# Attention steps of a two-layer mixer block: output banks, placement of weight splits, gates on GpSimd and an earlier first reciprocal

## What is computed

```
p = norm(x) @ w_in ; split: a (u, v, z), b (q, k, v, z), c (q, k, v, o, z, gates)
a: gelu(u) * (w_s @ layer_norm(gelu(v)) + b_s) * silu(z)
b: softmax(rope(norm(q)) . rope(norm(k)) * scale) @ v * silu(z)     8 heads, 2 kv heads
c: h = chunkwise mLSTM in both directions; norm(h) * g_head * sigmoid(o) * silu(z)
x = x + mod * (concat(a, b, c) @ w_out)
```

## Time and profile before

| | us |
|---|---|
| median of 3 runs | 1150.38 (1149.53 to 1152.26) |
| the profiled execution | 1150.57 |
| its span | 1148.6 |
| PE busy | 1093.4 (95%) |
| VectorE, ScalarE, GpSimd busy | 722.2, 590.7, 130.0 |
| mean granted clock of PE | 0.987 |
| attention of layer 0 | about 211 to 292 |
| attention of layer 1 | about 464 to 508 |

### The profile page before, as it was taken

The page is one execution under the profiler, slowest core; times in us unless marked ns, Lnnn a source line. Parts: engine busy times, 40 slices in busy tenths (PEclk is TensorE's granted clock), DMA queues, the critical chain, the costliest instruction groups (busy, mean ns, idle before and its releaser), DMA issues.

```text
span 1148.6 us, 19921 instructions
## 1 busy us (share of the span) xinstructions
PE 1093.4 (95%) x8128; PEld 958.1 (83%) x8128; DVE 722.2 (63%) x1227; ACT 590.7 (51%) x969; POOL 130.0 (11%) x156
## 2 busy tenths in 40 slices
PE   3999999999989999889999999999998999999998
PEld 1787888766767989579888999999997789999997
DVE  4546557376434667766866667666676667766764
ACT  5343666445233567656556555444465536544443
POOL 0000000044020000233223100000012321000000
PEclk9999999999898999989999999999999999999999
DMA  9732112177420433014433345555543233555451
GB/s 371 268 137 79 68 43 74 41 278 270 147 74 1 160 144 116 33 55 157 179 125 114 144 147 221 184 185 182 184 149 119 101 115 143 200 187 200 182 187 54
DMA packets 24426, 167.01 MB, mean 145 GB/s; under 512 B 2832, under 2 KB 3216, under 8 KB 4752
## 3 DMA queue, kind: packets, MB, share of 16 engines
q1 hardware_dynamic: 24336, 165.74, 39.4%
HBM read 164.68 MB, written 1.05 MB: 144 GB/s over the span
## 4 chain that ended last, share of the span: by engine, by line
PE 86%; DVE 5%; ACT 4%; issue 2%; POOL 1%; DMA 1%; SPq 0%; DVEq 0%; ACTq 0%; POOLq 0%
PE bank L426 24%; PE bank L427 23%; PE bank L428 23%; DVE wlo L420 2%; ACT whi L405 2%; PE bank L464 2%; PE bank L1373 2%; PE bank L1506 1%; PE bank L1526 1%; PE bank L1516 1%; PE bank L1400 1%; PE bank L1391 1%; DMA raw<-in_stream 1%; PE bank L479 1%; PE bank L2455 1%
## 5 line engine op out<-in xcount | busy, mean ns | idle before, releaser
L426 PE MATMUL bank<-OPH,whi 128*128 128x256 f32 (+1 forms) x1716 | 526.5, 307 | 5.8 <-DVE wlo L420 3.4
L427 PE MATMUL bank<-OPL,whi 128*128 128x256 f32 (+1 forms) x1716 | 516.7, 301 | 0.0
L428 PE MATMUL bank<-OPH,wlo 128*128 128x256 f32 (+1 forms) x1716 | 516.5, 301 | 0.0
L420 DVE TENSOR_TENSOR wlo<-raw,whi 128x1024 fp32r<-128x1024 f32 x256 | 305.3, 1234 | 109.5 <-ACT whi L405 109.3
L426 PEld LDWEIGHTS bank<-OPH,whi 128*128 128x128 f32 x1716 | 329.3, 192 | 27.8 <-issue 7.6
L427 PEld LDWEIGHTS bank<-OPL,whi 128*128 128x128 f32 x1716 | 329.4, 192 | 12.5 <-issue 1.7
L428 PEld LDWEIGHTS bank<-OPH,wlo 128*128 128x128 f32 x1716 | 329.2, 192 | 11.5
L405 ACT ACTIVATE whi<-raw 128x1024 fp32r<-128x1024 f32 x256 | 255.6, 1049 | 103.8 <-PE bank L428 103.8
L426 PE MATMUL bank<-whi,OPH 128*128 128x256 f32 (+1 forms) x272 | 89.2, 328 | 0.0
L427 PE MATMUL bank<-wlo,OPH 128*128 128x256 f32 (+1 forms) x272 | 87.3, 321 | 0.0
L428 PE MATMUL bank<-whi,OPL 128*128 128x256 f32 (+1 forms) x272 | 87.1, 320 | 0.0
(11 more groups left out here) (284 smaller groups left out, 1167.1 us busy)
## 6 DMA issues: line engine op xcount, KB each, us to landing
raw<-in_stream SPq DMA_DIRECT2D x147, 1024.0 KB, 4.8
PROJ<-in_stream SPq DMA_DIRECT2D x5, 1024.0 KB, 14.9
X<-in_x_in SPq DMA_DIRECT2D x4, 512.0 KB, 6.3
C<-in_con SPq DMA_DIRECT2D x1, 1477.5 KB, 9.1
out<-PROJ SPq DMA_DIRECT2D x4, 256.0 KB, 2.0
WST<-in_w_s SPq DMA_DIRECT2D x2, 256.0 KB, 5.0
PROJ<-in_last_gain SPq DMA_DIRECT2D x1, 512.0 KB, 5.7
BS<-in_b_s SPq DMA_DIRECT2D x1, 256.0 KB, 5.3
```

The source lines that it names most:

```text
L420: nc.vector.tensor_tensor(c.w[1][:, part], c.raw[:, part], c.w[0][:, part].bitcast(F32), ALU.subtract).then_inc(*raises(c.lo[h]))
L426: nc.tensor.matmul(out, w[0], x[0], start=start, stop=False, skip_group_check=skip)
L427: nc.tensor.matmul(out, w[0], x[1], start=False, stop=False, skip_group_check=skip)
L428: return nc.tensor.matmul(out, w[1], x[0], start=False, stop=stop, skip_group_check=skip)
```

## The change

1. The last weighted sums go to score banks: `last_outs` gives blocks 14 and 15 of layer 0 banks 2 and 3, and blocks 5 and 6 of layer 1 banks 2 and 3.
2. Splits of the output projection: in layer 0 to s + 0.5 in step 15 as before, to s + 1 behind the whole of step 17, to s + 2 behind the whole of step 20 (the last). In layer 1 to s + 2 behind the whole of step 11 (before: inside step 7); step 12 is the last.
3. The recurrent gates: cz x co is done by GpSimd (`join_gates`), in layer 0 after norm(2), in layer 1 after norm(0). `gate` is then one product for each j. In layer 0 the two stand behind step 3 and behind step 4; in layer 1 both in `between` of step 1, as one instruction each that reads the bank and multiplies by g_head and by the joined gates; `give` is dropped there.
4. `invert_first` puts the reciprocal of layer 1's block 0 into step 0, ahead of the gmlp gate.

```diff
-                if n >= self.steps - 2:
-                    split(e, self.after.s + (n - self.steps + 3) / 2)
+                if n == self.steps - 2:
+                    split(e, self.after.s + 0.5)
...
+                self.last_outs, self.inverted = {}, 0
...
-                    self.O.append(OPAIR.take("pe", ("dve",)))
+                    self.O.append(self.last_outs.get(i, OPAIR).take("pe", ("dve",)))
...
+            def invert_first(self):
+                self.inverted = 1
+                stage(f"{self.name}_first").dve = lambda e: self.invert(e, 0)
...
-                if 1 <= j <= self.n:
+                if self.inverted < j <= self.n:
                     self.invert(e, j - 1)
...
-                self.ready = [[("c_gated", l, j)] for j in range(2)]
+                self.ready = [self.bank[j].freed if l else [("c_gated", l, j)] for j in range(2)]
...
+            def join_gates(self):
+                st, l, n = stage(f"recurrent{self.l}_gates"), self.l, self.n
+
+                def pool(e):
+                    for point in due(e, self.pr.ready("cz", "co")):
+                        e.wait_ge(*point)
+                    for j in range(2):
+                        z, o = proj(CZ + j)[:, 0, 0:n], proj(CO + j)[:, 0, 0:n]
+                        nc.gpsimd.tensor_tensor(z, z, o, ALU.mult).then_inc(*raises(("c_gates", l, j)))
+
+                st.pool = pool
...
-            def gate(self):
+            def gate(self, js=(0, 1)):
                 st, l, n = stage(f"recurrent{self.l}_gate"), self.l, self.n
 
                 def dve(e):
-                    for j in range(2):
-                        for point in due(e, self.bank[j].freed, self.pr.ready("cz", "co")):
+                    for j in js:
+                        z = proj(CZ + j)[:, 0, 0:n]
+                        for point in due(e, self.bank[j].full if l else self.bank[j].freed, ("c_gates", l, j)):
                             e.wait_ge(*point)
-                        z, o = proj(CZ + j)[:, 0, 0:n], proj(CO + j)[:, 0, 0:n]
-                        nc.vector.tensor_tensor(z, z, o, ALU.mult).then_inc(*raises(("c_gates", l, j)))
-                        e.wait_ge(*when(("c_gates", l, j)))
-                        nc.vector.tensor_tensor(z, z, self.h[j], ALU.mult).then_inc(*raises(("c_gated", l, j)))
+                        if l:
+                            nc.vector.scalar_tensor_tensor(z, self.bank[j].mem[:, 0:n], vec("g_head", 2 * l + j), z,
+                                                           ALU.mult, ALU.mult).then_inc(*raises(self.bank[j].read["dve"]))
+                        else:
+                            nc.vector.tensor_tensor(z, z, self.h[j], ALU.mult).then_inc(*raises(("c_gated", l, j)))
...
-                between = {0: lambda: job("co_0"), 1: lambda: job("co_1"), 3: mo.gate}
+                between = {0: lambda: job("co_0"), 1: lambda: job("co_1"), 2: mo.join_gates}
+                after = {3: lambda: mo.gate((0,)), 4: lambda: mo.gate((1,))}
             else:
+                after = {}
...
-                between = {0: lambda: (job("co_0"), gm.mix(), mo.turn(), mo.give(), gm.gate()), 2: mo.gate,
+                between = {0: lambda: (job("co_0"), gm.mix(), mo.turn(), mo.join_gates(), at.invert_first(), gm.gate()), 1: mo.gate,
                            4: lambda: weights_ahead(wo_chunks[0].s + 1)}
...
+            at.last_outs = {at.n - 2: banks[2], at.n - 1: banks[3]} if l == 0 else {at.n - 3: banks[2], at.n - 2: banks[3]}
...
-            else:
-                between[at.n - 1] = lambda: weights_ahead(wo_chunks[0].s + 2)
-            if l == 0:
-                between[mod.steps] = lambda: weights_ahead(wo_chunks[0].s + 1.5)
-                between[mod.steps + 1] = lambda: weights_ahead(wo_chunks[0].s + 2)
...
+                if j in after:
+                    after[j]()
+                if l == 0 and j == at.n + 1:
+                    weights_ahead(wo_chunks[0].s + 1)
+                if j == at.steps - 1 - l:
+                    weights_ahead(wo_chunks[0].s + 2)
```

## The result

The changed kernel took 1137.95 us in the median of 4 runs (1137.61 to 1139.13), the kernel before 1149.95 beside it (4 runs, 1148.65 to 1152.26): ratio 0.9897, 95% interval 0.9886 to 0.9909. The forecast was 1138.7. The profiled execution took 1138.01 with a span of 1136.2, mean granted clock 0.993 for 0.987.

A forecast was written before the change was run, and what follows sets the result against it. PE was taken as the bound, busy 1093.4 of 1148.6 us, leaving waits and half-clock matmuls to shorten. Terms 2.35 + 2.1 + 0.4 + 2.6 + 4.4 = 11.85 off 1150.57 gave 1138.7; 8-in-10 range 1135.5 to 1144.5.

The forecast's parts named there:

- End of layer 0, score banks and split: Layer 0's end: with score banks and the moved split, the projection starts at 289.3 instead of 291.65, 2.35 us gained.
- Covered: Projections: gates' reads of banks 2 and 3 end long before the third and fourth job fill them, so cost nothing.
- Clock there: Layer 0's projection: the clock holds through 1.5 us of idleness, 2.1 us gained, bounds 0 and 2.1.
- Rival 1: The clock falls all the same at one of the two ends, costing 2.1 to 2.6 us: 1140.8 to 1141.3; chance 0.2.
- Gates of layer 0: Layer 0's steps: cz x co on GpSimd removes PE's wait for the row copy, 0.4 us gained, bounds +0.4 and -0.5.
- Start of layer 1: Layer 1, scores(0) to scores(5): early norm(0) and fused gates bring scores(5) 2.6 us sooner, bounds 2.0 and 2.9.
- the 2.0 end of the range: Start of layer 1: only 2.0 us gained if GpSimd and VectorE hold each other up at every pair.
- End of layer 1: Layer 1's end: projection starts 4.9 us sooner, 0.5 lost at the last operand, 4.4 gained; bounds 2.0 and 4.9.
- Rival 2: GpSimd's joins and norms hold up VectorE, so 2.6 and 0.4 go: 1141.7, with the clock too 1144; chance 0.1.
- Rival 3: Both ends: weighted sums wait for evictions of the transposes instead, and both clocks fall: 1147 to 1148; chance 0.04.
- Rival 4: Both projections: VectorE trails and every chunk makes PE wait one split, 2.36 us, 19 us in all: 1157.6; chance 0.03.

The follow-up runs named there:

- b3: The changed kernel without the first reciprocal at once (`invert_first` left out): 1142.85 us, ratio 0.9928 to the kernel before.
- a3: The kernel before with only the recurrent gates joined on GpSimd and fused, without the first reciprocal at once: 1148.80 us, ratio 0.9986.
- d2: The kernel before with only the first reciprocal at once: 1149.85 us, ratio 0.9996.
- d1: The changed kernel without the first reciprocal at once, with layer 1's joins ahead of norm(0) on GpSimd: 1138.30 us, ratio 0.9892.
- c1: The changed kernel with layer 1's split of chunk 1 behind the very last step: 1137.11 us, ratio 0.9885 to the kernel before.
- a1: The kernel before with only the last weighted sums moved to score banks: 1146.21 us, ratio 0.9961.
- b2: The changed kernel with the output projection's splits placed inside the steps as before: 1143.98 us, ratio 0.9939 to the kernel before.
- a4: The kernel before with the recurrent gates joined on GpSimd and fused, plus the first reciprocal at once: 1145.62 us, ratio 0.9959.

## Why the prediction was right, and where its reasons were not

**End of layer 0, score banks and split.** Size and date are right: 2.35 forecast, 2.23 measured, with ScalarE's eviction, the upper half and the lower half in the order forecast. What failed is the step that puts the gain on the banks, "weigh(14) no longer needs gate(12), nor weigh(15) gate(13)". The gates came late because a lower half stood ahead of them; the moved split takes that away by itself. Splits alone have all 4.4 us of layer 0, banks alone 2.4 (1.4 of it up to the start of the projection), and both no more than splits. The passage *Covered* had a step wrong too: the gates' reads of banks 2 and 3 are not over long before they matter, for the projection's first product waits for gate(14), 0.1 us.

**Clock there.** 2.1 forecast, 1.98 measured, clock 1.00 in both windows. But b3 had the same instructions and the same piece of 1.66 us, and its clock fell to 0.50, at a cost of 1.7 us. So the reason given, that PE had worked through 2.80 us at full clock, does not carry the term: the same piece holds in one execution and falls in another, and that it held in the measured one was in part luck. The first rival, by the Trainium skill, "TensorE: Matmul & The Clock Gate", Part 4, would have the transposes of turn(15) count for nothing and the clock fall. The two outcomes after the same 0.7 us of transposes, 1.2 us of weighing and 1.66 us of idleness neither bear the rule out nor refute it; no run isolates the transposes.

**Gates of layer 0.** 0.4 forecast, 0.27 measured, the wait at L479 gone. The 512-column joins took 1.49 us in the mean, for the 1.47 estimated. The remaining VectorE product beside one took 1.75 us. Its twin took 0.72 beside GpSimd's norm(3), and there it was GpSimd that took longer: 1.63 us for two products that took 1.19 where no such product ran (timelines of VectorE and of GpSimd):

```profile
235.09 1.75 DVE L2309 TENSOR_TENSOR PROJ<-PROJ 128x512 f32<-128x512 f32 x1
...
238.63 0.72 DVE L2309 TENSOR_TENSOR PROJ<-PROJ 128x512 f32<-128x512 f32 x1
```
```profile
238.19 1.63 POOL L1581 TENSOR_TENSOR TILE<-TILE,STAT 128x256 f32<-128x256 f32 x2 [1.90 <-DVE STAT L1572]
```

**Start of layer 1.** 2.6 forecast, 2.86 measured. "What is late next is the fused gate itself" holds: turn(0) waits for it (L2306) and comes 5.20 us after the end of exps(0), for 6.87 before, 1.67 sooner where 1.43 was forecast. The step that was missing is GpSimd's order of work: the forecast has norm(0) and then the joins and prices them, but not that the fused gate depends on the reciprocal through that queue. With the reciprocal in place this costs nothing; without it, it costs more than the whole gain of this stretch (23.77 and 23.66 us in a3 and b3, for 23.16 before). The early reciprocal that seemed the source of the gain is worth 0.8 us of the stretch alone and nothing that the time shows (d2), and another order of GpSimd's queue replaces it (d1).

**Contention.** The products of two SBUF operands beside GpSimd did slow down. The fused ones ran when GpSimd was done with the joins (466.60 + 1.66 = 468.26), so this kernel does not test them (timeline of VectorE, layer 1; 0.86 for two, 0.43 each):

```profile
465.85 0.96 DVE L1755 TENSOR_TENSOR PROJ<-PROJ,TILE 128x256 f32<-128x256 f32 x1
...
467.18 0.50 DVE L1755 TENSOR_TENSOR PROJ<-PROJ,TILE 128x256 f32<-128x256 f32 x1
...
468.80 0.86 DVE L2306 SCALAR_TENSOR_TENSOR PROJ<-bank,V,PROJ 128x256 f32<-128x256 f32 x2
```

L1755 took 0.42 both times in b3, where GpSimd was idle. The fused product is tested in b3: the first ran beside the second join and took 0.48 us, the second, with GpSimd idle, 0.48 as well. The 0.5 us lost in the first lies on the path to the fused gate at most in part, and the 2.0 end of the range was not reached. With the rule of the Trainium skill, "SBUF — State Buffer", Who interferes with whom, the trace agrees on both kinds of product.

**End of layer 1.** 4.9 forecast to the start of the projection, 4.98 measured; 0.5 to be lost at the last operand, 0.40 measured, and c1 shows it is the moved split. Norm(7) follows norm(6) directly. Again the split carries all of it; that weigh(5)'s bank gives anything is not shown, for the 0.5 of the banks alone lies within what this end varies by itself. The prediction put some 3.0 of the 4.9 down to the half clock. That was too much: a3 has the end as before, but at clock 1.00, and is 1.95 shorter, so the split is worth some 3.0 at full clock (12.39 to 9.35).

**Rivals.** Rival 1 (clock) did not occur in the changed kernel's two profiles, but did in b3's, with layer 0 unchanged. Rival 2 (GpSimd as the brake) did not occur in this kernel but is what b3 and a3 show, through the order of a queue rather than through slow products. Rival 3 (renamed waits) is true of the banks without the splits (a1, b2). Rival 4 (VectorE trailing in the projections) did not occur: the only wait in layer 1's projection is the 0.40, and layer 0's has none behind its start.

**Luck** had a part in two places. The clock at the end of layer 0, 2 of the 12 us, held in this execution and need not have. And the stretches outside happened to bring 0.66 in this profile, beside own terms that sum to 11.74 for 11.85.

## What to carry to other kernels

When several waits sit at one spot, look for the one piece of work queued ahead of all their releasers, here a weight split of 1.2 or 2.4 us that nobody needed yet; moving it behind them did what new buffers did only in part, and made them needless. When work moves to a third engine, write out each engine's queue in order and follow the dependency through all of them: the joins behind norm(0) behind a late reciprocal turned a gain of 2.9 us in this stretch into a loss of 0.5. Price parts in pairs: the joins alone lose 0.6 us of the stretch (a3), the reciprocal alone gains 0.8 (d2), and together they gain 2.9 (a4).

## What was not expected of the hardware

- What idleness does to the clock can't be told from the pieces of idleness. The same piece of 1.66 us between the same instructions left it at 1.00 in four profiled executions and brought 0.50 in a fifth (b3). The same piece of 2.20 us at the end of layer 1 brought 0.50 before and left 1.00 in a3; the one difference there is a piece some 4 us ahead, 0.52 before and 0.25 in a3, but d2 has 0.52 as before and fell less (0.69 for 0.55). A piece of 2.80 us left 1.00, one of 1.99 (a1) brought 0.65 over 290.50 to 292.00, one of 3.99 (b3) brought 0.50. So length alone does not say it; what does stays open. A term that rests on the clock holding is a chance and not a sum.
- The two joins of layer 1 took 1.66 us in the changed kernel, with VectorE's products beside them, and 1.41 in b3, where VectorE stood and waited for them: the delay goes both ways.
- The clock moves in stretches that no kernel touches. About the first norm it was 0.66 before (340.4 to 350.4), 0.83 after and 0.70 in the repeat (both 335 to 345); in one stretch of mla attention 1.00, 0.75 and 1.00. Each is worth 1 to 2 us, as much as single terms of the sum, so single parts were judged by distances between rows and not by the total. Of these distances too, those that hold a projection or an end of layer 1 carry such a clock.
